# A hybrid SSM and attention layer on one core: input projections in another order, with gate tiles in the scan and in the attention

## The chip, the core and the metric

One NeuronCore of a Trainium2 chip runs the whole program. The metric is device time in microseconds (us) of one execution, the median of three. The engines are TensorE (PE; its weight loads are PEld), VectorE (DVE), ScalarE (ACT), GpSimd (POOL) and SyncE (SP). They run their own instruction streams and meet at semaphores. ACT and SP also issue the DMAs.

## What is computed

A prompt of 512 tokens and 8 sample sequences of 8 tokens pass through one layer with the same weights: 576 tokens of width 1024.

```
h = rms_norm(x, w)
z, xBC, dt, q, k, v, gate_ssm, gate_attn = split(h @ w_in)     # 2048|4096|32|1024|256|256|1024|1024
u = silu(causal_conv4(xBC)); xs, B, C = split(u)
y = ssd_scan(xs, softplus(dt), A, B, C)          # chunks of 128, one more for the samples
y = (y + xs * d_skip) * silu(z)
A_out = group_rms_norm(y, 8 groups) @ w_ssm_out
B_out = window_attention_with_sinks(rope(q), rope(k), v) @ w_attn_out
x = x + (sigmoid(gate_ssm) * A_out + sigmoid(gate_attn) * B_out) @ w_out
x = x + peer_ffn(rms_norm(x))                     # 16384 experts, top 16 of 8 heads
out = rms_norm(x)
```

The conv state, the SSM state and the key and value windows are outputs too.

## The kernel before

Activations lie transposed, 128 channels in the partitions and 576 tokens in the free dimension. A *projection tile* is 128 output columns of a weight matrix: 8 pieces of 128 x 128, each multiplied as high and low halves in fp32r (high by high, high by low, low by high), in two column halves of 288, so 48 matmuls into two PSUM banks. `project(n, p, ...)` issues it; `n` counts weight tiles and `p` the PSUM pair (parity) and its uses.

Each weight tile goes through two buffers: SP loads it into `raw` (512 KB), ACT copies the high part (`high(n)`, `whi`), POOL subtracts for the low part (`low(n)`, `wlo`). `high(n)` waits until PE is done with tile `n-2`, and everything behind it in ACT's program waits with it. The order of the weight tiles in memory is the order of use, given by the constants `N_DT`, `N_XBC`, `N_QKV`, `N_ATT`, `N_Z`, `N_SSM`, `N_OUT`.

No scheduler is at work: each engine's order is the order in which its function is written. The stages ahead of the expert network are:

1. norm, the dt tile, then 32 conv tiles (`N_XBC`). ACT copies a tile out of PSUM (`fill`), DVE does the four taps (`conv`, L1499 to L1515), ACT the silu.
2. the scan `ssd(c)` over four prompt chunks and one sample chunk. In a chunk DVE stages the chunk's operands, PE forms the cumulated decays (L570, L571), turns six blocks (L586), and then goes through 8 groups: `front(g)` spreads the decays (L611) and multiplies C by B (L614); `back(g)` makes the chunk state (L626) and the outputs (L637, L640). Between them are ACT's exponentials (`exps`) and DVE's masks and products. In the sample chunk `new_states` (L598) and 8-column outputs (L647) take the place of the state products, and ACT moves 16 states of 512 KB in and out.
3. 12 tiles of q, k and v, with the rotation on ACT and DVE (`swap`, `rope`).
4. the attention of the prompt, 16 units (`scores` L702, softmax on DVE and ACT, `turn` L713, `take` on ACT, `values` L725), then four pairs of samples (`attend_pair`).
5. 16 tiles: for each of 8 blocks the attention gate and the attention's output projection.
6. 16 z tiles, each with a silu on ACT and a product with y on DVE (L1801), the group sums (L794), the reciprocals (L1806) and the normalized outputs in halves (`yn`, L1809 to L1815).
7. 24 tiles: for each of 8 blocks the ssm gate and two tiles of `w_ssm_out`, merged on DVE; then 8 tiles of `w_out`.

The expert network behind it takes over half of the time and has the same instructions in both kernels.

## Time and profile before

| | us |
|---|---|
| median of 3 runs (2968.07 to 2972.53) | 2969.11 |
| the profiled execution's own time | 2970.44 |
| its span, first to last instruction | 2968.6 |
| conv tiles, 45.0 to 262.7 | 217.7 |
| four prompt chunks, 281.2 to 446.0 | 164.8 |
| sample chunk, 446.0 to 609.7 | 163.7 |
| q, k, v and the values' turn, 609.7 to 694.9 | 85.2 |
| prompt attention, 694.9 to 822.4 | 127.5 |
| sample attention, 822.4 to 870.6 | 48.2 |
| gates, outputs of both branches, 870.6 to 1254.4 | 383.8 |
| the rest (w_out and the expert network) | 1714.2 |

TensorE is busy for 2768.2 us of the span (93%), DVE for 1888.6, ACT for 915.0 and POOL for 683.4. A busy TensorE is not one at its peak: small matmuls count as busy for their latency, and it runs at one of two clocks, 2.4 GHz (shown as 1.00) or 1.2 GHz (0.50). The seven stages above were cut at the first or last instruction that belongs to them.

### The profile page before, as it was taken

How to read it: one execution, taken by the hardware profiler on the slowest of the kernel's cores; microseconds unless marked ns; L12 is line 12 of the kernel's file. 1: busy time of each engine (PE TensorE's matmuls, PEld its weight loads, DVE VectorE, ACT ScalarE, POOL GpSimd, SP SyncE). 2: the span in 40 equal slices, each digit the busy share in tenths (PEclk: the TensorE clock that was granted, in tenths of full speed). 3: DMA queues.
4: the chain of work that ended last, by engine and by line, in shares of the span. 5: the costliest groups of instructions: out<-in, count | busy, mean ns of one | idle time of the engine just before them, and what ended most of it. 6: DMA issues, size and time to landing. Idle time of an engine off the chain costs nothing.

```text
span 2968.6 us, 46810 instructions
## 1 busy us (share of the span) xinstructions
PE 2768.2 (93%) x15762; PEld 2406.5 (81%) x15762; DVE 1888.6 (64%) x3749; ACT 915.0 (31%) x1527; POOL 683.4 (23%) x345
## 2 busy tenths in 40 slices
PE   6997789997779999989999999999998999999997
PEld 5996668995369999988888888887887888888886
DVE  5998874325620582227799998884667777755554
ACT  2333440044412441123333345553221211211211
POOL 1332000021003324323345423333441111100000
PEclk9998885588869999999999999999999999999999
DMA  3221002321002212312334335457999888866662
GB/s 120 78 78 62 1 0 101 117 96 50 1 27 85 78 64 78 108 66 93 113 132 146 141 149 197 179 191 278 335 342 292 290 289 289 274 196 193 190 196 83
DMA packets 253899, 430.31 MB, mean 145 GB/s; under 512 B 146912, under 2 KB 149600, under 8 KB 252384
## 3 DMA queue, kind: packets, MB, share of 16 engines
q1 hardware_dynamic: 53712, 195.58, 18.7%
q10 hardware_dynamic: 181680, 166.60, 17.0%
q0 software_dynamic: 18432, 67.12, 6.7%
q8 instruction: 48, 0.79, 0.1%
q14 instruction: 27, 0.22, 0.0%
HBM read 349.46 MB, written 81.71 MB: 145 GB/s over the span
## 4 chain that ended last, share of the span: by engine, by line
PE 47%; issue 45%; POOL 6%; DVE 1%; DMA 1%; ACTq 0%; POOLq 0%; ACT 0%; DVEq 0%; SPq 0%
PE ps L955 24%; PE ps L854 19%; POOL wlo L488 6%; PE ps L925 4%; DMA raw<-wt 1%; ACTq L1402 0%; PE ps L534 0%; POOLq L490 0%; DVE y_out L2107 0%; DVE rinv L2105 0%; ACTq L1399 0%; PE ps L905 0%; ACT whi L1021 0%; DVE onehot_i L2004 0%; DVE wlo L2025 0%
## 5 line engine op out<-in xcount | busy, mean ns | idle before, releaser
L488 POOL TENSOR_TENSOR wlo<-raw,whi 128x1024 fp32r<-128x1024 f32 x213 | 539.4, 2533 | 1502.9 <-ACT whi L1021 1502.9
L1021 ACT ACTIVATE whi<-raw 128x1024 fp32r<-128x1024 f32 x373 | 394.9, 1059 | 1478.3 <-PE ps L955 544.7
L854 PE MATMUL ps<-h_hi,whi 128*128 128x512 f32 x1024 | 403.3, 394 | 6.7 <-DVE wlo L2025 4.8
L955 PE MATMUL ps<-act_hi,whi 128*128 128x512 f32 x1024 | 399.4, 390 | 9.1 <-DVE act_lo L1450 9.1
L854 PE MATMUL ps<-h_lo,whi 128*128 128x512 f32 x1024 | 399.8, 390 | 0.0
L854 PE MATMUL ps<-h_hi,wlo 128*128 128x512 f32 x1024 | 399.5, 390 | 0.0
L955 PE MATMUL ps<-act_lo,whi 128*128 128x512 f32 x1024 | 399.2, 390 | 0.0
L955 PE MATMUL ps<-act_hi,wlo 128*128 128x512 f32 x1024 | 399.1, 390 | 0.0
L2025 DVE TENSOR_TENSOR wlo<-raw,whi 128x1024 fp32r<-128x1024 f32 x160 | 196.1, 1225 | 306.3 <-ACT whi L1021 306.3
L525 PE MATMUL ps<-h_hi,whi 128*128 128x288 f32 x1360 | 303.0, 305 | 25.5 <-DVE h_lo L1450 18.9
L525 PE MATMUL ps<-h_hi,wlo 128*128 128x288 f32 x1360 | 296.2, 300 | 0.0
L525 PE MATMUL ps<-h_lo,whi 128*128 128x288 f32 x1360 | 296.1, 300 | 0.0
L525 PEld LDWEIGHTS ps<-h_hi,whi 128*128 128x128 f32 x1360 | 223.2, 193 | 36.3 <-issue 21.2
L955 PEld LDWEIGHTS ps<-act_hi,whi 128*128 128x128 f32 x1024 | 192.7, 188 | 49.5 <-issue 9.5
L854 PEld LDWEIGHTS ps<-h_hi,whi 128*128 128x128 f32 x1024 | 193.0, 189 | 46.8 <-ACT tmp L1317 5.2
L854 PEld LDWEIGHTS ps<-h_hi,wlo 128*128 128x128 f32 x1024 | 192.9, 188 | 40.5
L955 PEld LDWEIGHTS ps<-act_hi,wlo 128*128 128x128 f32 x1024 | 192.8, 188 | 40.2
L955 PEld LDWEIGHTS ps<-act_lo,whi 128*128 128x128 f32 x1024 | 192.8, 188 | 40.1
L854 PEld LDWEIGHTS ps<-h_lo,whi 128*128 128x128 f32 x1024 | 193.1, 189 | 38.6
L525 PEld LDWEIGHTS ps<-h_hi,wlo 128*128 128x128 f32 x1360 | 224.0, 193 | 0.0
L525 PEld LDWEIGHTS ps<-h_lo,whi 128*128 128x128 f32 x1360 | 223.9, 193 | 0.0
L2004 DVE TENSOR_SCALAR onehot_i<-consts_sb,expert_turned 128x128 f32<-128x128 f32 x512 | 205.8, 461 | 0.0
(282 smaller groups left out, 4068.2 us busy)
## 6 DMA issues: line engine op xcount, KB each, us to landing
raw<-wt SPq DMA_DIRECT2D x245, 512.0 KB, 3.2
raw<-pv SPq DMA_DIRECT2D x128, 512.0 KB, 4.5
activations<-tmp ACTq DMA_DIRECT2D x128, 256.0 KB, 2.0
gates_dense<-g_block ACTq DMA_DIRECT2D x8, 4096.0 KB, 13.1
g_tile<-gates_dense ACTq DMA_DIRECT2D x128, 256.0 KB, 3.6
gelu<-activations ACTq DMA_DIRECT2D x128, 256.0 KB, 4.1
state_s<-s_in ACTq DMA_DIRECT2D x16, 512.0 KB, 4.2
ssm_s<-state_s ACTq DMA_DIRECT2D x16, 512.0 KB, 2.9
```

What stands on the lines that cost most here:

```text
L488: pool.tensor_tensor(lo, raw[n.par][:, :], hi.bitcast(F32), ALU.subtract).then_inc(split_ready, 1)
L525: mm = pe.matmul(PS[2 * p.par + h][:, 0:HT], w[slot][:, k, :], x[:, k0 + k, h * HT:(h + 1) * HT], start=first and k == 0 and w is whi and ...
L854: mm = pe.matmul(PS[2 * p.par][:, :], w[slot][:, k, :], x[:, k, 0:SEQ], start=k == 0 and w is whi and x is HH, stop=k == KD - 1 and w is wlo)
L925: mm = pe.matmul(PS[4 + k][:, q * P:(q + 1) * P], OJ[buf][:, q, :], AI[buf][:, q, :], start=True, stop=True)
L955: mm = pe.matmul(PS[d][:, :], w[s][:, d, :], x[b][:, :], start=first and w is whi and x is ACH, stop=last and w is wlo)
L1021: act.activation(whi[slot][:, :, :].rearrange("p k c -> p (k c)"), raw[slot][:, :], ACT.Copy)\
L2004: ins = dve.tensor_scalar(AI[buf][:, q, :], iota, EJT[:, 0, tok], EJT[:, 2, tok], ALU.is_equal, ALU.mult)
L2025: dve.tensor_tensor(lo, raw[slot][:, :], hi.bitcast(F32), ALU.subtract).then_inc(split_ready, 1)
```

## The change

The 100 projection tiles between the dt tile and `w_out` are the same, in another order:

- The 12 tiles of q, k and v stand among the conv tiles: two conv tiles, one of these, twelve times, then 8 conv tiles. Rotated q and k, and v, are stored in a DRAM tensor `qkv_turned`, and loaded back by four DMAs ahead of the attention.
- The 32 gate inputs (16 z, 8 attention gates, 8 ssm gates) become *side tiles*. They use PSUM banks 0 and 1 only, and are issued in two halves of 24 matmuls (`side(n, j, part)`). ACT copies each to SBUF and stores it in a DRAM tensor `gate_inputs`.
- 20 side tiles stand in the scan, four in each chunk: a half behind the second and the fourth of the turned blocks, and a half behind the outputs of each of the groups 1 to 6. Two stand behind the scan, four in the prompt attention (a half behind every second `turn`), two in the sample attention (a half behind each pair), four behind the attention's output projection.
- To free the banks, a prompt chunk's decays use banks 2 and 3, the C by B product bank 6 alone, and the chunk state bank 7 alone; the chunk state now follows the group's outputs. The attention's scores use banks 2 and 3 alone.
- All silu(z) and products with y are done between the scan and the attention, from tiles loaded back. The group sums and reciprocals stand beside the attention's output projection, and the normalized outputs (`yn`) behind all of them. The gates are loaded back and put through the sigmoid.

```diff
+            for k in range(6):
+                mixed(Idx(N_MIX + k))
+            with pe.Fori(1, MIXES) as r:
+                for k in range(6):
+                    mixed(Idx(N_MIX + k, r, 6))
+            for k in range(CX - 4 * MIXES):
+                mixed(Idx(N_XTAIL + k))
+            def side(n, j, part):
+                if part == 0:
+                    pe.wait_ge(split_ready, n.v + 1)
+                    if not isinstance(j, int) or 0 < j < SIDES_2:
+                        pe.wait_ge(side_used, j)
...
+                slot = slot_of(n)
+                for k in range(4 * part, 4 * part + 4):
+                    for w, x in ((whi, HH), (whi, HL), (wlo, HH)):
+                        for h in range(2):
+                            mm = pe.matmul(PS[h][:, 0:HT], w[slot][:, k, :], x[:, k, h * HT:(h + 1) * HT],
...
                     mm.then_inc(turned, 1)
+                    if q in (1, 3):
+                        fill(q // 2)
...
-                        pe.wait_ge(cb_ready, u - 1)
                         pe.wait_ge(seg_ready, u - 1)
                         pe.wait_ge(ec_ready, u - 1)
...
                     mm.then_inc(y_ready, 1)
+                    if not sample:
+                        if not start or g >= 1:
+                            pe.wait_ge(cs_used, u)
+                        pe.matmul(PS[7][:, 0:4 * HP], BTK[:, g, :], XDD[:, 4 * g * HP:4 * (g + 1) * HP],
+                                  start=True, stop=True).then_inc(cs_ready, 1)
...
                     back(g)
+                    if 1 <= g <= 6:
+                        fill(g + 1)
...
+            for j in range(SIDES_1, SIDES_1 + 2):
+                for part in range(2):
+                    side(Idx(N_SIDE + j), j, part)
+            pe.wait_ge(qkv_in, 16 * 4)
...
                 turn(u)
+                if u % 2 == 0:
+                    j = SIDES_1 + 2 + u // 4
+                    side(Idx(N_SIDE + j), j, u // 2 % 2)
                 if u < UNITS - 2:
                     scores(u + 2)
...
+            for m in range(KD):
+                project(Idx(N_AO + m), Idx(P_AO + m), OH, OL)
+                group_sums(m)
+            for j in range(SIDES_2, SIDES):
+                for part in range(2):
+                    side(Idx(N_SIDE2 + j - SIDES_2), j, part)
+            pe.wait_ge(side_used, SIDES)
+            def ssm(n, p, first=False):
+                if first:
+                    pe.wait_ge(yn_done, NG // 2)
+                project(n, p, YH, YL, last=False)
+                if first:
+                    pe.wait_ge(yn_done, NG)
+                project(plus(n, 1), p, YH, YL, k0=KD, first=False)
...
+            def side(n, j, k, half):
+                high(plus(n, 2))
...
+                for h in range(2):
+                    ins = act.activation(SIDE[k][:, h * HT:(h + 1) * HT], PS[h][:, 0:HT], ACT.Copy)
+                ins.then_inc(side_used, 1)
+                act.wait_ge(side_used, j + 1)
+                act.dma_start(dram(side_dram, j), SIDE[k][:, :]).then_inc(side_out[k], 16)
...
+            for m in range(CI):
+                if m + 3 < CI:
+                    if m:
+                        act.wait_ge(yz_ready, m)
+                    load_z(m + 3)
+                act.wait_ge(z_in[m % 4], 16 * (m // 4 + 1))
+                act.activation(ZB[m % 4][:, :], ZB[m % 4][:, :], ACT.Silu).then_inc(zs_ready, 1)
+                if m == CI // 2:
+                    side_at(Idx(N_SIDE + SIDES_1 + 1), SIDES_1 + 1)
...
+            for m in range(CI):
+                dve.wait_ge(zs_ready, m + 1)
+                x = UX[:, m, :]
+                dve.tensor_tensor(x, x, ZB[m % 4][:, :], ALU.mult).then_inc(yz_ready, 1)
+            dve.wait_ge(qkv_in, 16 * 4)
...
+            for m in range(KD):
+                att(m)
+                rinv(m)
...
+            for g in range(NG):
+                yn(g)
```

TensorE in a prompt chunk, one of the groups 1 to 6, before (`seg`, `xdt` and `state` are operands of the outputs; two rows of outputs stand for eight):

```order
L611 MATMUL ps<-consts_sb,da_chunk 128x128 x4
L614 MATMUL ps<-u_bc,st_b 128x128
L626 MATMUL ps<-xdt_decayed,b_tok 128x256
L637 MATMUL ps<-seg_107,xdt 64x128
L640 MATMUL ps<-c_decayed_109,state 64x128
```

and now:

```order
L667 MATMUL ps<-consts_sb,da_chunk 128x128 x4
L678 MATMUL ps<-u_all,st_b 128x128
L695 MATMUL ps<-seg_114,xdt 64x128
L698 MATMUL ps<-c_decayed_116,state 64x128
...
L714 MATMUL ps<-xdt_decayed,b_tok 128x256
L595 MATMUL ps<-h_hi,whi_51 128x288 x2
L595 MATMUL ps<-h_lo,whi_51 128x288 x2
L595 MATMUL ps<-h_hi,wlo_53 128x288 x2
```

The chunk state (L626, now L714) moved behind the outputs, and 24 matmuls of a half side tile (L595) follow it, ahead of the next group's decays.

ScalarE behind the scan's last state store, before (the rotation's tables and the masks, then the first tile of q):

```order
L1142 DMA cos_sin<-ropes 128x1152
L1143 DMA mask_prompt<-amask 128x512
L1144 DMA mask_sample<-smask 128x1536
L1021 ACTIVATE whi_52<-raw_50 128x1024
L1154 ACTIVATE rope_swap_138<-ps 32x288 x8
```

and now (`z_148` to `z_151` are the four buffers for the z tiles):

```order
L1275 DMA q<-qkv_turned 128x8x576
L1276 DMA mask_prompt<-amask 128x512
L1277 DMA mask_sample<-smask 128x1536
L1280 DMA z_148<-gate_inputs 128x576
...
L1085 ACTIVATE whi_52<-raw_50 128x1024
L1178 ACTIVATE side_64<-ps 128x288 x2
L1181 DMA gate_inputs<-side_64 128x576
L1280 DMA z_151<-gate_inputs 128x576
L1293 ACT_TABLE_LOAD
L1293 ACTIVATE z_148<-z_148 128x576
L1280 DMA z_148<-gate_inputs 128x576
L1293 ACTIVATE z_149<-z_149 128x576
```

The loads of q and the masks stand ahead of the first z tile, and from then on a load and a silu take turns, 16 times.

TensorE in the prompt attention, before (a `turn`, the scores of the unit after next, the values):

```order
L713 MATMUL ps<-consts_sb,scores_142 128x128 x8
L702 MATMUL ps<-k_pad,q 128x256 x4
L725 MATMUL ps<-p_turned,v_tok 64x512 x2
```

In every second unit a half side tile of 24 matmuls now stands between the `turn` and the scores.

## Rows read from the trace of the kernel before

**Rows 1.** Busy time by stage: us, each engine's busy us (x instructions), clock, DMA.
```profile
45.00:262.70 217.70, 211.44 (x1548) 207.82 (x1546) 200.24 (x346) 75.20 (x160) 78.47 (x32) 0.99 0.21 75
281.20:446.00 164.80, 130.06 (x1009) 102.97 (x1009) 124.25 (x293) 69.48 (x200) 0.00 (x0) 0.82 0.01 2
446.00:609.70 163.70, 153.69 (x942) 141.64 (x942) 65.58 (x108) 12.34 (x50) 0.00 (x0) 0.50 0.30 105
609.70:694.90 85.20, 80.91 (x592) 80.43 (x591) 26.08 (x50) 46.18 (x96) 28.68 (x12) 0.97 0.28 98
694.90:822.40 127.50, 93.92 (x320) 50.05 (x321) 80.74 (x162) 50.33 (x176) 0.00 (x0) 0.83 0.04 12
822.40:870.60 48.20, 33.53 (x272) 24.99 (x272) 17.54 (x84) 8.57 (x40) 0.00 (x0) 0.54 0.08 23
870.60:1254.40 383.80, 378.56 (x2752) 374.03 (x2752) 141.62 (x125) 115.40 (x167) 134.90 (x55) 0.99 0.22 75
```
**Rows 2.** Timeline, ScalarE's high parts of two weight tiles: start, us, operation, idle before.
```profile
887.14 1.06 ACT L1021 ACTIVATE whi<-raw 128x1024 fp32r<-128x1024 f32 x1 [3.27 <-PE ps L525]
893.54 1.06 ACT L1021 ACTIVATE whi<-raw 128x1024 fp32r<-128x1024 f32 x1 [5.34 <-PE ps L525]
```
**Rows 3.** Timeline of TensorE, the second prompt chunk.
```profile
321.84 0.64 PE L570 MATMUL ps<-da_chunk,consts_sb 128*128 128x32 f32 x2 [3.43 <-DVE da_chunk L1559]
...
331.18 2.05 PE L611 MATMUL ps<-consts_sb,da_chunk 128*128 128x128 f32 x8 [0.97 <-DVE b_tok L1577]
...
337.38 0.45 PE L637 MATMUL ps<-seg,xdt 128*64 128x128 f32 x4 [1.67 <-DVE c_decayed L1605]
...
347.44 1.16 PE L611 MATMUL ps<-consts_sb,da_chunk 128*128 128x128 f32 x8
...
349.55 0.45 PE L637 MATMUL ps<-seg,xdt 128*64 128x128 f32 x4 [0.30 <-DVE c_decayed L1605]
...
350.62 1.16 PE L611 MATMUL ps<-consts_sb,da_chunk 128*128 128x128 f32 x8
```
**Rows 4.** Busy time in two single microseconds: the seventh number is the clock.
```profile
320.00:321.00 1.00, 0.00 (x0) 0.00 (x0) 1.00 (x2) 0.00 (x0) 0.00 (x0) 0.96 0.00 0
614.00:615.00 1.00, 1.00 (x8) 1.00 (x8) 0.00 (x0) 0.00 (x0) 0.00 (x0) 0.77 0.70 194
```
**Rows 5.** Timeline of TensorE, one group of the sample chunk.
```profile
474.46 1.97 PE L611 MATMUL ps<-consts_sb,da_chunk 64*128 64x64 f32 x8
...
476.95 7.19 PE L598 MATMUL ps<-xdt_decayed,b_by_seq 64*128 64x128 f32 x32
...
492.90 1.97 PE L611 MATMUL ps<-consts_sb,da_chunk 64*128 64x64 f32 x8
```
**Rows 6.** Timeline, one product of y and silu(z) without POOL, one with it.
```profile
1090.07 0.75 DVE L1801 TENSOR_TENSOR u_x<-u_x,tmp 128x576 f32 x1
...
1091.89 2.34 POOL L488 TENSOR_TENSOR wlo<-raw,whi 128x1024 fp32r<-128x1024 f32 x1 [4.01 <-ACT whi L1021]
1092.57 2.28 DVE L1801 TENSOR_TENSOR u_x<-u_x,tmp 128x576 f32 x1 [1.75 <-ACT tmp L985]
```
**Rows 7.** Timeline of ScalarE: a DMA issue among eight, and the silu of a z tile.
```profile
695.22 0.47 ACTq L1170 DMA_DIRECT2D v_cache<-vc  x1
...
1003.30 0.69 ACT L985 ACTIVATE tmp<-ps 128x288 f32<-128x288 f32 x2
```
**Rows 8.** The page's DMA list: tensor, queue, count, KB each, us from issue to landing.
```profile
gates_dense<-g_block ACTq DMA_DIRECT2D x8, 4096.0 KB, 13.1
```
**Rows 9.** TensorE's waits in the two attentions: total, times, longest.
```profile
PE ps L753 <- DVE q_sample L1748: 5.0, 4, 1.9
```
**Rows 10.** Timeline of DVE: the last but one reciprocal, and the normalization of a group.
```profile
1094.77 3.74 DVE L1806 RECIPROCAL rinv<-rinv 128x576 f32<-128x576 f32 x1
...
1098.70 1.55 DVE L1809 SCALAR_TENSOR_TENSOR yn<-u_x,params_sb,rinv 128x576 f32<-128x576 f32 x2 [0.19 <-DVE rinv L1806]
...
1102.02 0.76 DVE L1815 TENSOR_TENSOR y_lo<-yn,y_hi 128x576 f32 x1
```

**Rows 11.** Timeline of TensorE, the sums of one group in the z stage.
```profile
1002.14 2.10 PE L794 MATMUL ps<-sqz,ones 128*128 128x288 f32 x8
```

More of the change, by code:

```diff
@@ L330, in build @@
         ML = put(m_r, "m_lo", [P, KD, T], F32R)
+        RG = put(over(r2, 18432), "group_rinv", [P, NG, T])
         z_r = over(x_r)
@@ new lines, in value @@
+            def value(n, j, k):
+                high(plus(n, 2))
+                act.wait_ge(rope_done, 9 + k)
+                if k == 0:
+                    store_turned(9, 1)
+                halves(RS[k], n, ACT.Copy).then_inc(slot_used[n.par], 1)
+                act.wait_ge(slot_used[n.par], n.half + 1)
+                act.dma_start(dram(qkv_dram, j), RS[k][:, :]).then_inc(q_out[k], 16)
+            for k in range(2):
+                conv_pair(Idx(N_MIX + 3 * k), 2 * k, first=k == 0)
+                swap(Idx(N_MIX + 3 * k + 2), k, k, first=True)
@@ L1158, in _, with load_z @@
-            for k in range(2):
-                swap(Idx(N_QKV + k), k, k, first=True)
-            with act.Fori(1, 5) as i:
-                for k in range(2):
-                    swap(Idx(N_QKV + k, i, 2), i * 2 + k, k)
-            for k in range(2):
-                n = Idx(N_QKV + 10 + k)
-                high(plus(n, 2))
-                halves(VT[k], n, ACT.Copy).then_inc(slot_used[n.par], 1)
+            def load_z(m):
+                act.dma_start(ZB[m % 4][:, :], side_dram[m]).then_inc(z_in[m % 4], 16)
@@ new lines, in _, with load_gate, ssm_gate @@
+            for m in range(KD):
+                high(Idx(N_AO + m + 2))
+                z_std(m)
+                if m < KD - 1:
+                    z_squares(m + 1)
+            for j in range(SIDES_2, SIDES):
+                side_at(Idx(N_SIDE2 + j - SIDES_2), j)
+            def load_gate(m, k):
+                act.dma_start(TMP[k][:, :], dram(side_dram, m + (CI + KD))).then_inc(gate_in[k], 16)
+            def ssm_gate(n, m, k, half, first=False, last=False):
+                act.wait_ge(gate_in[k], half * 16 + 16)
+                act.activation(TMP[k][:, :], TMP[k][:, :], ACT.Sigmoid).then_inc(sgate_ready, 1)
+                for j in range(2):
+                    high(plus(n, 2 + j))
+                if not first:
+                    act.wait_ge(merged, m)
+                if not last:
+                    load_gate(m + 1, 1 - k)
```

462 lines of the change are left out of this document (242 added, 220 removed).

## Prediction, made before the kernel was run

> **What bounds the kernel now.** I read the table by stage first [rows 1]. In every stage with projection tiles TensorE is busy nearly throughout, at the full clock. Two neighbouring tiles start 893.54 - 887.14 = 6.40 us apart [rows 2], which is 48 matmuls of 0.133; a half side tile is 3.2 us. The conv stage runs at 217.7 / 33 = 6.6 us a tile, because DVE is busy for 200 of its 217.7 us. TensorE loses time elsewhere: in the prompt chunks it is busy for 130 of 164.8 us, in the attentions for 94 of 127.5 and 34 of 48.2, and the sample chunk, where it is busy nearly always, ran at the lower clock, 0.50 [rows 1]. The number of matmuls doesn't change. So the change can win only what a side tile costs less in the scan and the attentions than 6.40 us, and it loses what new waits it makes. The stages are followed one by one.
>
> **Conv stage.** 12 tiles are moved in: +76.8. A rotated tile is light for DVE, whose conv work no longer sets the pace: 24 conv tiles at 6.4 instead of 6.6, so -4. **+73.**
>
> **Prompt chunks.** A group takes 350.62 - 347.44 = 3.2 us [rows 3], set by the chain through ACT and DVE. TensorE shows 0.30 us idle in it (ahead of 349.55), and 0.2 to 0.3 more lie in its latencies; its matmuls need about 2.6. So a half tile there is hardly hidden: 2.6 + 3.2 = 5.8 us a group, in six groups 34.8. ACT and DVE need under 4 us from a group's decays to its outputs, so they keep up with that. The chunk's start is better cover. From the first matmul (321.84) to the first decays (331.18) are 9.3 us at the lower clock, with TensorE waiting for DVE. With two half tiles in it I work out 17.4: at the full clock 0.6 + 6 x 0.9 + 6.4 = 12.4, 2.7 for the cold first part, and 2.3 for b_tok's copy. The clock there was seen to fall after TensorE had been idle since 318.4 (0.96 within 320 to 321 [rows 4]), and that gap stays; the dense half tile should raise it. Then 4.9 from the decays to the first output (337.38 - 331.18 = 6.2 with decays at the lower clock, 1.3 less at the full one), 1.4 and 0.9 for the outputs of groups 0 and 7, and 5.3 for DVE's staging: 3.6 as now, and 1.7 because POOL now works in the scan. A product on DVE that took 0.75 us alone took 2.28 when it began 0.7 us into a POOL subtraction of 2.34 [rows 6]: DVE stands until POOL is done. Sum 17.4 + 4.9 + 1.4 + 34.8 + 0.9 + 5.3 = 64.7 a chunk, 259 for four, against 164.8: **+94**, where 16 tiles elsewhere cost 102. Bounds: 60 a chunk (+75) if no start is cold, 68 (+107) if POOL and the cold clock meet at both ends.
>
> The Trainium skill ("SBUF — State Buffer", "Who interferes with whom") says that DVE is held up by GpSimd only where it reads two SBUF operands or runs in a two-port mode. The row agrees, since u_x and tmp both lie in SBUF. By that rule the copies of b_tok out of PSUM would go free, and the four chunks would take some 9 us less; no row here tells.
>
> **Sample chunk.** A group takes 492.90 - 474.46 = 18.4 us [rows 5] at the lower clock, all of it TensorE. At 1.2 GHz 288 columns take 0.24 us, so a half tile of 24 matmuls is 5.8 us and a group 24.2. What the clock does decides this stage. The row of the projection behind the scan says that the clock rises about 4.6 us after dense work began (begun at 609.7, 0.77 within 614 to 615 [rows 4]). So it should rise in or behind each half tile and hold through the decays and the 7.2 us of new states, both cold work of 9.5 that then takes half, and drop somewhere in the 8-column outputs, which have no such row. Bounds: no gain (24.2 a group) and full clock throughout (12.1). I take 8 us saved, 16.2 a group, nearer to what the continuous new states suggest. Sample chunk: 163.7 + 2 (two half tiles in its start, one of them behind a wait) - 4 (group 0 warm) + 4 (POOL) - 6 x 2.2 = 152.5: **-11**.
>
> **Between scan and attention.** Before: 85.2, of which 76.8 are tiles. Now two tiles are left (12.8) and two other chains are longer. The last state's store must land (3.5 us after the scan, as now). Then ACT issues 4.6 MB for q, k, v and the masks ahead of the first z tile; 4 MB took 13.1 us in this trace [rows 8], so the first z arrives about 20 us after the scan. From there silu, product, load take turns: ACT may load tile m+3 only when DVE has multiplied m-1. So each of 12 tiles costs 0.69 + 0.75 + 0.47 + 0.1 = 2.0 us [rows 6, 7], and with the last four, a side tile in the middle and two POOL subtractions the loop takes 32. Copies of k and v behind it add 3: 20 + 32 + 3 = 55, against 85.2. **-30**, so of 10 tiles' 64 us more than half is given back as an idle TensorE. Bounds 45 and 62.
>
> **Prompt attention.** The half tile falls in the time in which TensorE waits; 127.5 - 93.9 = 34 us are idle [rows 1] and 25.6 come in. The chain goes from DVE's softmax to ACT and back, and scores are asked for some 5 us after the turn, so most is hidden. Not hidden: the first, at the lower clock (+3), and four POOL subtractions that catch DVE on the chain (4 x 1.6). **+9**, bounds 0 and +26.
>
> **Sample attention.** A half tile at the lower clock (5.8, some of it raised: 5.1), of which the wait for the queries covers 5.0 / 4 [rows 9], four times with the last uncovered: 3 x 4 + 5 + 2 for POOL. **+19**, bounds +10 and +26.
>
> **Outputs.** 28 tiles leave: -179.2. New waits: 2 for the copy of the last side tile; 4.4 at the third output tile, whose `high` stands in ACT behind the loads of 2.4 MB of gates and two sigmoids; 2 for the last side tile; and `yn`. That starts when the eighth reciprocal is done, 6.6 us after the last output tile (2.9, and 3.74 [rows 10]), and takes 8 x 4.1 = 33 us (1098.70 to 1102.78 [rows 10]), plus some 5 x 2.2 for POOL: 51 (2.9 is the sum on TensorE and the root on ACT). TensorE needs the second half of it after 1.9 + 25.6 + 2 + 6.4 = 36. So it waits 15. That makes 23 us of waits. The same account of the stage before leaves 10: 383.8 less 56 tiles of 6.40 and eight group sums of 1.9 (2.10 with the last one's latency [rows 11]), which stand in both. So +13. **-166**, bounds -178 and -158.
>
> Behind that nothing changes. Sum: 73 + 94 - 11 - 30 + 9 + 19 - 166 = **-12**. The profiled execution's span is 2968.6 and its own time 2970.4, 1.3 above the median; so 2969.1 - 12 = **2957**.
>
> **Rivals.**
>
> *The clock stays low in the sample chunk* (slower than before). If the half tiles don't raise it, or it drops at once behind them, six groups cost 24.2 instead of 16.2: +48, 3005; half of that gives 2981. For it: 164 us in which TensorE was busy 94% of the time at 0.50 [rows 1], new states of 7.2 us without a rise among them. Against it: rows 4, where a projection raised the clock in less time than the half tile has. It decides against the change from a group of 18.2 us on (-12 + 6 x 2 = 0).
>
> *The clock stays high through the sample chunk.* Groups near 13 us: -25, **2932**. The Trainium skill ("TensorE: Matmul & The Clock Gate", "What's actually happening") says that activity releases the throttle and a sustained busy engine gets the full clock. By that this would hold. The sample chunk of this trace disagrees, since it is busy and at 0.50; the rule needs a narrower sense of busy than the profile's.
>
> *DVE and ACT are less late than worked out.* If the z loop overlaps (1.3 us a tile) and `yn` isn't held by POOL, -8 and -11: **2938**. For it: my loop adds up latencies that the trace shows only in other places.
>
> *The change does nothing where it says most*: in the prompt chunks the half tiles find no room (0.5 us a group). That is in the sum; were the starts as bad as the groups, +8, 2965.
>
> **Chances.** Forecast 0.50 (its own range 2940 to 2972), clock low 0.22 (2972 to 3010), clock high 0.13, less late 0.15. The likeliest gives 2957. The range reaches from 2920, for two of the better cases together, to 2995, short of the full price of the low clock. A measurement here tells about 0.2% (6 us) from no change. Faster by more than that (below 2963): 0.28 of the forecast's 0.50, and nearly all of the two better cases: 0.60. Within 0.2%: 0.16. Slower: 0.24.
>
> **What would show it.** Right: a prompt chunk of 62 to 67 us; the granted clock of the sample chunk between 0.6 and 0.9 and its length near 152; the first scores some 55 us behind the scan with TensorE idle for about 40; a single wait of TensorE of about 15 us for y_lo. Wrong: a clock of 0.50 in the sample chunk, groups above 6.5 us in the prompt chunks (then a chain through ACT, which now waits for tiles among its exponentials, is the bound), or a prompt attention over 150 us.

## The result, and the profile after

The changed kernel takes **2984.5 us** (median of 6 runs, 2977.2 to 2993.7) against 2969.3 of the kernel before; the ratio is 1.0051, 95% interval 1.0036 to 1.0065. So it is slower by half a per cent, where 2957 was forecast. The profiled execution has a span of 2984.0, 15.4 more than that of before. One execution in the slow state (4805.5 us, in experiment 1) is left out of all that follows.

The stages of the new kernel, as [rows 1] shows those of the old one (busy us and number of instructions of TensorE, its weight loads, VectorE, ScalarE, GpSimd; granted clock; DMA share; GB/s):

```profile
45.00:338.10 293.10, 285.59 (x2119) 285.19 (x2118) 206.58 (x396) 123.07 (x257) 105.83 (x44) 0.98 0.28 91
338.10:351.10 13.00, 1.09 (x15) 0.81 (x13) 11.24 (x26) 4.25 (x7) 2.34 (x1) 0.70 0.27 93
351.10:606.20 255.10, 221.93 (x1776) 207.14 (x1776) 133.23 (x293) 96.16 (x248) 37.74 (x16) 0.93 0.15 50
606.20:797.90 191.70, 168.14 (x1134) 156.92 (x1134) 67.04 (x108) 18.95 (x62) 9.40 (x4) 0.64 0.32 110
797.90:849.00 51.10, 18.74 (x111) 18.27 (x110) 15.49 (x26) 15.18 (x23) 4.71 (x2) 0.67 0.66 225
849.00:984.40 135.40, 113.00 (x514) 75.48 (x516) 81.19 (x162) 57.82 (x189) 9.44 (x4) 0.90 0.11 35
984.40:1052.30 67.90, 51.09 (x369) 43.17 (x369) 19.85 (x86) 11.89 (x46) 2.96 (x2) 0.67 0.10 29
1052.30:1269.00 216.70, 201.63 (x1408) 196.85 (x1408) 111.88 (x107) 60.69 (x80) 70.55 (x28) 0.96 0.30 96
```

Set against [rows 1], stage by stage:

| stage | before | after | change | forecast |
|---|---|---|---|---|
| conv tiles | 217.7 | 293.1 | +75.4 | +73 |
| wait ahead of the scan | 18.5 | 13.0 | -5.5 | 0 |
| four prompt chunks | 164.8 | 255.1 | +90.3 | +94 |
| sample chunk | 163.7 | 191.7 | **+28.0** | **-11** |
| between scan and attention | 85.2 | 51.1 | -34.1 | -30 |
| prompt attention | 127.5 | 135.4 | +7.9 | +9 |
| sample attention | 48.2 | 67.9 | +19.7 | +19 |
| outputs | 383.8 | 216.7 | -167.1 | -166 |
| the rest | 1714.2 | 1715.0 | +0.8 | 0 |

(The wait ahead of the scan lies between 262.7 and 281.2 in the kernel before, between two rows of [rows 1].) One stage missed its forecast by 39 us. All others together came out 12 us below theirs. The question for the runs is what happened in the sample chunk.

One group of the sample chunk, in TensorE's timeline of the changed kernel (start, us, operation; in brackets the idle time before it and what ended it), to be read beside [rows 5]:

```profile
676.71 0.85 PE L595 MATMUL ps<-h_hi,whi 128*128 128x288 f32 x2
...
682.16 1.10 PE L667 MATMUL ps<-consts_sb,da_chunk 64*128 64x64 f32 x8
...
683.45 4.12 PE L655 MATMUL ps<-xdt_decayed,b_by_seq 64*128 64x128 f32 x32
687.50 0.33 PE L695 MATMUL ps<-seg,xdt 64*64 64x64 f32 x2
692.06 1.88 PE L705 MATMUL ps<-c_decayed,state_s 128*64 128x8 f32 x16 [4.24 <-DMA state_s<-s_in]
...
698.68 1.87 PE L705 MATMUL ps<-c_decayed,state_s 128*64 128x8 f32 x16
705.98 1.10 PE L667 MATMUL ps<-consts_sb,da_chunk 64*128 64x64 f32 x8
```

The half tile (676.71 to 682.16) starts a pair of matmuls every 0.48 us up to 681.20, and only its last three pairs are closer (0.26 to 0.36 us). The decays then take 1.10 instead of 1.97 and the new states 4.12 instead of 7.19. But the first 8-column outputs wait 4.24 us for a load of states, an idle time that the kernel before doesn't have, and run at 1.88 as ever. The clock over the same stretch, in three pieces (columns as above):

```profile
676.40:680.80 4.40, 4.40 (x21) 4.38 (x21) 3.94 (x6) 0.00 (x0) 0.00 (x0) 0.50 0.00 0
680.80:687.80 7.00, 6.95 (x53) 6.25 (x52) 2.93 (x6) 3.14 (x9) 2.35 (x1) 0.96 0.34 119
687.80:704.80 17.00, 12.76 (x89) 12.30 (x89) 4.57 (x8) 0.00 (x0) 0.00 (x0) 0.51 0.36 123
```

So of a group of 23.8 us (682.16 to 705.98) some 7 are at 2.4 GHz. The waits of TensorE in the chunk (total, times, longest), and the page's DMA list (count, KB each, us to landing), which has 4.2 us for these loads in the kernel before:

```profile
PE ps L705 <- DMA state_s<-s_in: 19.3, 5, 5.1
```

```profile
state_s<-s_in ACTq DMA_DIRECT2D x16, 512.0 KB, 5.9
```

### The profile page after: what moved, and what is told of

Same layout as the page of the kernel before. It is cut to its first block, busy times and chain, and to the rows that moved or that the text cites. A ratio compares the mean times of both kernels' runs of the same rounds, so it can differ in the third digit from the quotient of the medians.

```text
span 2984.0 us, 46325 instructions
## 1 busy us (share of the span) xinstructions
PE 2744.6 (92%) x15762; PEld 2406.5 (81%) x15762; DVE 1862.8 (62%) x3749; ACT 920.8 (31%) x1542; POOL 684.2 (23%) x345
## 3 DMA queue, kind: packets, MB, share of 16 engines
q10 hardware_dynamic: 194128, 192.56, 19.3%
## 4 chain that ended last, share of the span: by engine, by line
PE 46%; issue 45%; POOL 6%; DVE 1%; DMA 1%; ACTq 0%; POOLq 0%; ACT 0%; DVEq 0%; SPq 0%
PE ps L1018 23%; PE ps L917 19%; POOL wlo L508 6%; PE ps L988 4%; DMA raw<-wt 1%; ACTq L1530 0%; PE ps L554 0%; POOLq L510 0%; DVE y_out L2234 0%; DVE rinv L2232 0%; PE ps L968 0%; ACT whi L1085 0%; DVE onehot_i L2131 0%; ACTq L1527 0%; DVE wlo L2152 0%
## 5 line engine op out<-in xcount | busy, mean ns | idle before, releaser
L917 PEld LDWEIGHTS ps<-h_hi,whi 128*128 128x128 f32 x1024 | 193.0, 189 | 47.5 <-ACT tmp L1445 5.4
L917 PEld LDWEIGHTS ps<-h_hi,wlo 128*128 128x128 f32 x1024 | 192.9, 188 | 40.5
L917 PEld LDWEIGHTS ps<-h_lo,whi 128*128 128x128 f32 x1024 | 193.1, 189 | 38.4
L545 PE MATMUL ps<-h_hi,whi 128*128 128x288 f32 x848 | 187.5, 303 | 28.4 <-DVE h_lo L1578 21.6
L545 PE MATMUL ps<-h_lo,whi 128*128 128x288 f32 x848 | 184.7, 300 | 0.0
L545 PE MATMUL ps<-h_hi,wlo 128*128 128x288 f32 x848 | 184.4, 300 | 0.0
L545 PEld LDWEIGHTS ps<-h_hi,whi 128*128 128x128 f32 x848 | 138.7, 192 | 34.4 <-issue 22.8
L545 PEld LDWEIGHTS ps<-h_lo,whi 128*128 128x128 f32 x848 | 139.8, 193 | 0.0
L595 PE MATMUL ps<-h_hi,whi 128*128 128x288 f32 x512 | 132.2, 344 | 8.3 <-issue 6.2
## 6 DMA issues: line engine op xcount, KB each, us to landing
activations<-tmp ACTq DMA_DIRECT2D x128, 256.0 KB
g_tile<-gates_dense ACTq DMA_DIRECT2D x128, 256.0 KB, 3.7
gelu<-activations ACTq DMA_DIRECT2D x128, 256.0 KB, 3.6
```

The lines of the kernel that those rows point to most:

```text
L545: mm = pe.matmul(PS[2 * p.par + h][:, 0:HT], w[slot][:, k, :], x[:, k0 + k, h * HT:(h + 1) * HT], start=first and k == 0 and w is whi and ...
L595: mm = pe.matmul(PS[h][:, 0:HT], w[slot][:, k, :], x[:, k, h * HT:(h + 1) * HT], start=k == 0 and w is whi and x is HH, stop=k == KD - 1 a ...
L917: mm = pe.matmul(PS[2 * p.par][:, :], w[slot][:, k, :], x[:, k, 0:SEQ], start=k == 0 and w is whi and x is HH, stop=k == KD - 1 and w is wlo)
```

## The experiments

Below, TensorE's work is called *cold* where it runs at 1.2 GHz and *warm* where it runs at 2.4. The theory after this reading: the sample chunk costs 39 us more than forecast since (a) the raised clock gives some 4 us a group and not 8, and (b) TensorE waits 19.3 us for states, because the half tile stands where it delays the new states, whose results must be stored before the buffer is loaded again, with three buffers in turn. The rival: the clock alone, or the half tiles as such, wherever they stand. (The reason given in (b) proved too narrow; what delays the loads is read from ScalarE's timeline in the part on the sample chunk below.)

### 1. The half tile ahead of the outputs

```
             new_states(g, 0)
+            if 1 <= g <= 6:
+                fill(g + 1)
             pe.wait_ge(mt_ready, u + 1)
...
                 back(g)
-                if 1 <= g <= 6:
-                    fill(g + 1)
```

> The changed kernel, but in groups 1 to 6 of the sample chunk the half side tile stands between the new states and the outputs instead of behind the outputs. Theory (place): the half tile then covers the loads of the states (waits of 4.24 + 1.77 + 5.09 + 3.62 + 4.60 = 19.3 us in the changed kernel), and it still raises the clock, now for the outputs in place of the decays and new states (about 4 us less a group either way). Groups of about 20 us instead of 22.7, sample chunk about 175 instead of 191.7, no wait for a state load; total about 2968. Rival (the clock alone): the 8-column outputs don't gain from the clock and the decays and new states are cold again: groups 18.4 + 5.8 = 24.2, total about 2993.

Measured: 2972.3 us (median of 9), 12 less than the changed kernel, ratio to the kernel before 1.0008 (0.9998 to 1.0018). The sample chunk takes 179.8 us, 12 less as well, with groups of 20.5 on average (637.72 to 740.47, five groups), and no wait for a load is left. Its TensorE timeline:

```profile
681.81 7.19 PE L655 MATMUL ps<-xdt_decayed,b_by_seq 64*128 64x128 f32 x32 [0.18 <-DVE state_s L1789]
...
694.41 1.10 PE L707 MATMUL ps<-c_decayed,state_s 128*64 128x8 f32 x16
...
697.27 1.87 PE L707 MATMUL ps<-c_decayed,state_s 128*64 128x8 f32 x16
```

New states are cold again (7.19), and the first two of the four pieces of outputs are warm or nearly so (1.10 and 1.25 instead of 1.87; in another group all four are): this is the duration at the full clock that no row of before had. The clock gives no more here (24.2 - 20.5 = 3.7 us a group) than where the half tile stood before (groups of 22.9 with 2.2 of wait in each on average, so 24.2 - 20.7 = 3.5), and the kernel is still 12 us faster. So the place of the half tile matters, through the loads, and the "clock alone" rival (2993) falls.

### 2. A fourth buffer for the states

```
+        S0.append(nc.alloc_sbuf_tensor_at("state_s3", [P, SB, P], F32, offset=tmp_at - 4096))
...
-                    if 1 <= v < 2 * NG - 2:
-                        act.wait_ge(s0_out[(v - 1) % 3], 16 * ((v - 1) // 3 + 1))
-                        load_states(v + 2)
+                    if 1 <= v < 2 * NG - 3:
+                        act.wait_ge(s0_out[(v - 1) % 4], 16 * ((v - 1) // 4 + 1))
+                        load_states(v + 3)
```

> The changed kernel with a fourth buffer for the sample states, each load issued one state earlier; nothing else moved. Theory: the waits of TensorE for state loads (19.3 us in five groups) go and nothing takes their place: all groups at about 21 us, sample chunk about 173, total about 2966. Rival: the loads are only slower because the weight tiles are loaded beside them, and one buffer more moves the wait to the stores or to DVE's updates: half or less of it goes, 2975 or more.

Measured: 2965.5 (median of 10), 19 less than the changed kernel, ratio to before 0.9986 (0.9973 to 0.9999). The chunk takes 169.8, the waits for loads fall from 19.3 to 5.4. TensorE in one group, and the clock of its two parts:

```profile
680.32 1.10 PE L668 MATMUL ps<-consts_sb,da_chunk 64*128 64x64 f32 x8
...
681.61 4.12 PE L656 MATMUL ps<-xdt_decayed,b_by_seq 64*128 64x128 f32 x32
...
685.91 1.10 PE L706 MATMUL ps<-c_decayed,state_s 128*64 128x8 f32 x16
...
690.18 1.88 PE L706 MATMUL ps<-c_decayed,state_s 128*64 128x8 f32 x16 [1.63 <-DMA state_s<-s_in]
```

```profile
680.32:688.80 8.48, 8.18 (x81) 7.45 (x80) 3.39 (x6) 3.13 (x9) 2.35 (x1) 1.00 0.62 181
688.80:699.00 10.20, 8.82 (x54) 8.65 (x55) 4.03 (x6) 0.00 (x0) 0.00 (x0) 0.51 0.35 137
```

The wait did two things. It stood between the new states and the outputs, and in some groups it kept the outputs out of the time at the full clock: in the changed kernel the clock stood at 1.00 for the first 3.0 and 2.9 us of the waits that end at 737.69 and 760.34, though only for some 0.2 us of the one shown above. With most of the wait gone, the first half of the outputs shown runs warm. The groups from 662.11 on take 18.2, 19.5, 18.2 and 19.6 us. That is a group of before with a half tile in it at nearly no cost. The chunk's remaining 6 us against 163.7 are mostly the first filled group, 24.2 (24.5 in the changed kernel). So the late loads do cost these 19 us, and (a) and (b) are not independent. But the edit adds a buffer and also issues each load one state earlier in ScalarE's program, and it doesn't tell which of the two was needed. The loads still take 5.9 us to land, against 4.2 in the kernel before: that they are slower is so, but it doesn't keep the gain away.

### 3. The sample chunk's tiles behind the scan

```
-                    if q in (1, 3):
+                    if q in (1, 3) and not sample:
                         fill(q // 2)
...
                         back(g)
-                        if 1 <= g <= 6:
-                            fill(g + 1)
...
-            for j in range(SIDES_1, SIDES_1 + 2):
+            for j in range(CI, SIDES_1 + 2):
                 for part in range(2):
                     side(Idx(N_SIDE + j), j, part)
```

(The half tiles of groups 1 to 6 are taken out of the sample chunk alone; ScalarE's part of the tiles moves too, three ahead of the z loop and three at its steps 2, 5 and 8.)

> The changed kernel with the four side tiles of the sample chunk moved behind the scan, where TensorE idles for 29.5 us waiting for the z loop and the copies of k and v: six tiles there instead of two. Theory: the sample chunk goes back to the 163.7 us of the kernel before (-28), and the stage behind it grows by less than 5 us since four tiles (25.6) fit into the idle time: about 2960. Rival: ScalarE, which takes the tiles' copies and high parts between the z tiles, stretches the z loop, and the stage grows by 15 or more: 2972 or more.

Measured: 2979.2 (median of 10), ratio to before 1.0030 (1.0018 to 1.0043). The sample chunk is nearly back, at 165.8, 26 less. The stage behind takes 74.3 instead of 51.1. The rival holds in its size, not in its reason. TensorE there:

```profile
803.15 0.50 PE L595 MATMUL ps<-h_hi,whi 128*128 128x288 f32 x2 [1.84 <-ACT side L1176]
813.12 0.51 PE L595 MATMUL ps<-h_hi,whi 128*128 128x288 f32 x2 [1.84 <-ACT side L1176]
```

A side tile costs 10.0 us here, not 6.4: all side tiles use the same pair of PSUM banks, so each waits for ScalarE to copy the one before, and after the idle time of 1.8 to 2.1 us the clock falls, just behind the start of the tile: for the tile begun at 783.20 it reads 0.50 in the microseconds from 784 to 786, and 1.00 from 787 on.

### 4. The same with two pairs of banks

```
+                    bank = (j + 1) % 2
+                    pe.wait_ge(side_used, j - 1)
...
-        mm = pe.matmul(PS[h][:, 0:HT], w[slot][:, k, :], x[:, k, h * HT:(h + 1) * HT],
+        mm = pe.matmul(PS[2 * bank + h][:, 0:HT], w[slot][:, k, :], x[:, k, h * HT:(h + 1) * HT],
```

> The kernel with the sample chunk's four side tiles moved behind the scan, and there the six tiles take turns between two pairs of PSUM banks. With one pair they started 10.0 us apart, since each waited 1.84 us for ScalarE's copy of the one before and then ran its first 3 us at the lower clock. Theory: back to back they take 6.4 each (some 40 us), the z loop and the copies of k and v end the stage again at about 52 us instead of 75.8: total about 2958. Rival: ScalarE's part of the tiles (a copy, a high part and a store, 2.1 us each, and its waits for them) stretches the z loop: still 65 us or more, 2970.

Measured: 2966.5 (median of 10), ratio 0.9985 (0.9976 to 0.9995), between the two forecasts. The six tiles now start at 774.21 and are done by 816, with one hole of 2.08 us (a low part that came late, as ScalarE made its high part late), but TensorE then waits longer:

```profile
774.21 0.82 PE L604 MATMUL ps<-h_hi,whi 128*128 128x288 f32 x2 [0.83 <-issue]
...
809.70 0.53 PE L604 MATMUL ps<-h_hi,whi 128*128 128x288 f32 x2 [2.08 <-POOL wlo L510]
...
835.28 3.78 PE L770 MATMUL ps<-k_pad,q 64*128 64x256 f32 x8 [17.40 <-DVE k_tok L1832]
```

The stage takes 61.9 (12 less than with one pair of banks, and 11 more than in the changed kernel), and what ends it is the z loop (by way of the copies of k and v), which runs on ScalarE in turns with the tiles' own work. Theory and rival are both right in part: TensorE had room for the tiles; ScalarE, whose timeline stops for each of them, did not.

### 5. No side tiles in the sample attention

```
-SIDES_1, SIDES_2 = 20, 28
+SIDES_1, SIDES_2 = 20, 26
...
                     attend_pair(i, h)
-                    j = SIDES_2 - 2 + i
-                    side(Idx(N_SIDE + j), j, h)
```

> The changed kernel with the two side tiles of the sample attention moved to the outputs stage. Theory: they cost 67.8 - 48.2 = 19.6 us where they are and 2 x 6.4 = 12.8 there: total about 7 less, 2978. Rival: the outputs stage hides part of them under the wait for y_lo (about 12 us less altogether, 2972), or the wait for the states' last stores was what they covered (no gain, 2984).

Measured: 2976.5 (median of 10), 8 less. By stage, in its profiled execution: the sample attention is back at 48.6, the outputs stage has 225.8 instead of 216.7, so 9 for two tiles; the rest lay in the wait of 6.3 for `y_lo`, which the changed kernel has there and this one has not.

```profile
974.80:1023.40 48.60, 33.40 (x272) 24.92 (x272) 18.04 (x87) 8.57 (x40) 0.00 (x0) 0.51 0.08 24
1023.40:1249.20 225.80, 215.04 (x1504) 210.25 (x1504) 109.63 (x107) 64.10 (x86) 73.95 (x29) 0.97 0.31 96
```

### 6. The pieces together

Four state buffers, no side tile in the sample attention, four tiles behind the scan in two pairs of banks:

```
-                    j = SIDES_1 + 2 + u // 4
+                    j = SIDES_1 + 4 + u // 4
                     side(Idx(N_SIDE + j), j, u // 2 % 2)
```

> The changed kernel with four state buffers, no side tile in the sample attention, and four side tiles behind the scan that take turns between two pairs of banks. Theory: the costs add up: -19 for the states, -19.6 for the sample attention, and the two more tiles behind the scan are hidden by the z loop: about 2946. Rival: the tiles behind the scan show (+8 or more), or the sample chunk's gain depends on where the clock stands: 2955 or more.

Measured: **2948.1** (median of 4, 2943.8 to 2953.9), ratio 0.9931 (0.9914 to 0.9949). The sample chunk takes 168.4, the stage behind it 57.0 (5.9 more than in the changed kernel, so the two further tiles do show there), the sample attention 48.6. In the sum the costs add up to what was forecast (2946), since the sample chunk's profile shows 23 less and not 19.

### 7. The normalization started earlier

```
                 rinv(m)
+                own.wait()
+                for k in range(2):
+                    x = UX[:, m * 2 + k, :]
+                    own.mark(dve.scalar_tensor_tensor(x, x, Q[:, Q_SNW + m * 2 + k:Q_SNW + m * 2 + k + 1],
+                                                      RG[:, m, :], ALU.mult, ALU.mult))
```

(And the last four side tiles in two pairs of banks, as in experiment 4.)

> As the kernel with four state buffers and no side tile in the sample attention, and besides the multiplication of yn by the reciprocal is done in place during the output tiles, where VectorE idles 3.7 us of every 8.3, and the last four side tiles take turns between two pairs of banks. Theory: yn is ready some 12 us earlier, the side tiles take 6.4 instead of 8.3 to 9.9 each, and TensorE reaches the wait for y_lo earlier: about 10 us less than without, 2936. Rival: VectorE is late for the output tiles now (a POOL subtraction makes a 1.55 us pair longer), and the tiles give the time back: 2946.

Measured: **2934.8** (median of 4, 2929.5 to 2941.1), ratio 0.9885 (0.9865 to 0.9906), 13 less than experiment 6. From the first output tile to the last matmul on y it takes 198.9 instead of 211.4. VectorE's pair does meet GpSimd, and 3.69 stands where 1.55 would, but the time for it is there (below). How much of the 13 is the norm's and how much the banks', no run separates.

```profile
1044.25 3.69 DVE L1948 SCALAR_TENSOR_TENSOR u_all<-u_all,params_sb,group_rinv 128x576 f32<-128x576 f32 x2
...
1083.20 1.55 DVE L1948 SCALAR_TENSOR_TENSOR u_all<-u_all,params_sb,group_rinv 128x576 f32<-128x576 f32 x2
```

### 8. Two half tiles a group

Experiment 7 with a half tile behind the new states and another behind the outputs:

```
             new_states(g, 0)
+            if 1 <= g <= 6:
+                fill(2 * g)
...
-                            fill(g + 1)
+                            fill(2 * g + 1)
```

> As the kernel with the early norm, with two half tiles a group in the sample chunk (one behind the new states, one behind the outputs: seven tiles there instead of four), three behind the scan and two in the outputs stage. Theory: the clock falls some 5 to 8 us after a half tile and rises 3 to 4 us into the next, so with half tiles this close it hardly falls: decays and new states 5.5, outputs 5.9, two half tiles 3.2 to 4 each, about 19 us a group, as long as now with one half tile; two tiles fewer later, -8 of 12.8 (the rest is wait for yn): about 2928. Rival: the clock falls in each piece all the same, or the state transfers (2 MB a group beside 0.5 MB of weights) set the pace: 22 us or more a group, 2945 or more.

Measured: 2938.8 (median of 4), ratio 0.9883 (0.9865 to 0.9902), no different from experiment 7. One group, and the clock of its two parts:

```profile
701.72 1.10 PE L677 MATMUL ps<-consts_sb,da_chunk 64*128 64x64 f32 x8
...
707.05 0.54 PE L605 MATMUL ps<-h_hi,whi 128*128 128x288 f32 x2
...
710.70 1.10 PE L717 MATMUL ps<-c_decayed,state_s 128*64 128x8 f32 x16
...
716.20 0.85 PE L605 MATMUL ps<-h_hi,whi 128*128 128x288 f32 x2
```

```profile
701.72:714.80 13.08, 13.03 (x127) 12.12 (x127) 3.39 (x6) 3.14 (x9) 2.35 (x1) 1.00 0.66 224
714.80:721.98 7.18, 7.18 (x39) 7.00 (x38) 4.03 (x6) 0.00 (x0) 0.00 (x0) 0.53 0.00 0
```

A group is 20.3 us with twice the projection work in it: all of decays, new states and the first half tile (3.4 us, not 5.8) run at the full clock, and the clock falls at the end of the outputs; the second half tile is cold (716.20 to 721.98) but for its last matmuls. So the forecast of the group (19) was nearly met, and no transfer sets the pace (TensorE has no wait for states in this run). What was wrong is what it would bring. The chunk is 9.8 longer than in experiment 7, and the two tiles fewer in the outputs stage give back only 3.8 of 12.8 (195.1 against 198.9), as `yn` ends at its own time. The stage behind the scan, with one tile less, took 59.7, not less: it is the z loop's.

### 9. The half tile ahead of the outputs in the prompt chunks

> The changed kernel with the half tile of groups 1 to 6 of the four prompt chunks ahead of the group's outputs instead of behind them. Theory: place matters only where TensorE waits; in the prompt chunks a group of 6.0 us is filled by its own work (2.8) and the half tile (3.2) without an idle moment, so nothing changes: within 3 us of the changed kernel. Rival: the place decides here as in the sample chunk, since the chain over ScalarE and VectorE (3.2 us a group before) gets the half tile as cover for the outputs rather than for the next decays: 0.3 to 0.5 us a group, 7 to 12 us less.

The edit is that of experiment 1, for the prompt chunks instead. Measured: 2979.5 (median of 7), ratio 1.0032 (1.0021 to 1.0044); the changed kernel, run again beside it, 2983.4. The four chunks take 256.0 us, against 255.1 in the changed kernel. The 4 us between the medians lie within the spread of either, and not in these chunks. The order is of no matter there.

### 10. z first

```
+            for m in range(3):
+                load_z(m)
             act.dma_start(KP[:, :, WIN:WIN + T], qkv_dram[8:10].rearrange("k p t -> p k t")).then_inc(qkv_in, 16)
...
+                if m < KD:
+                    act.dma_start(QT[:, m, :], qkv_dram[m]).then_inc(q_in, 16)
```

> As the kernel with the early norm, with the first z tiles loaded ahead of k, v, q and the masks, q loaded tile by tile between the steps of the z loop, and the side tiles' copies spread over the loop. Theory: the stage behind the scan is a chain that starts with 12 to 13 us of loads (4.6 MB ahead of the first z tile) and goes on with 16 steps of 2 us: with z first the loads lie beside the steps, and the first scores come about 45 us behind the scan instead of 57.8: total about 2923. Rival: the stage is bound by its bytes (some 11 MB): then the order doesn't matter, 2932 or more.

Measured: 2931.7 (median of 4, 2923.8 to 2938.6), ratio 0.9872 (0.9848 to 0.9896), 3 less than experiment 7, which four runs each don't separate. The stage takes 52.6 instead of 57.8, so 5 of the 13 us hoped for, and the sample chunk, which was not edited, 170.1 instead of 167.0. The first product comes 14 us behind the scan, but then a step takes 2.4 and not 1.9, since one more issue stands in it, and steps with a side tile 3.6; the DMA share rises from 0.66 to 0.75, which leaves the question of how near its bytes are to a bound open.

### 11. The changed kernel again

> The changed kernel once more, unedited, to stand beside the two others on the same chip: 2977 to 2994, median about 2984, as in its first six runs.

Measured: 2983.4 (median of 4, 2977.0 to 2983.8), as before. Its profiled execution has a span of 2975.2, and the 9 us less have a place: ScalarE's high parts in the conv stage come 6.24 us apart,

```profile
301.28 1.06 ACT L1085 ACTIVATE whi<-raw 128x1024 fp32r<-128x1024 f32 x1 [3.95 <-PE ps L545]
307.52 1.06 ACT L1085 ACTIVATE whi<-raw 128x1024 fp32r<-128x1024 f32 x1 [3.95 <-PE ps L545]
```

not 6.40, so the stage is 6 us shorter, and the sample chunk takes 186.2 instead of 191.7. In the executions of experiments 5 and 9, which leave this chunk as it is, it takes 185.5 and 188.7. So one profile tells its length to some 6 us only, and the 191.7 used above is the longest of the four; the gains of experiments 1 and 2 rest on the medians, 12 and 19 us. Experiments 4, 6, 7 and 8 ran on another chip than these; the kernel before took 2970.2 there, and 2970.4 and 2969.2 here.

## Why the prediction was wrong, step by step

**Conv stage: right.** +75.4 against +73. The steady tile was 6.40 with VectorE no longer behind. The wait ahead of the scan, which the prediction left as it was, fell from 18.5 to 13.0: VectorE is busy for 11.2 us of it, where it was for 16.6. That term was missing. (In the forecast, 24 tiles at 6.4 instead of 6.6 make -4.8, not -4.)

**Prompt chunks: right.** The chunks take 63.9, 63.3, 64.2 and 63.7 (64.7 forecast), a group 6.0 (5.8). TensorE has no idle row in a group:

```profile
588.22 1.05 PE L667 MATMUL ps<-consts_sb,da_chunk 128*128 128x128 f32 x8
...
589.43 0.45 PE L695 MATMUL ps<-seg,xdt 128*64 128x128 f32 x4
...
590.85 0.61 PE L595 MATMUL ps<-h_hi,whi 128*128 128x288 f32 x2
...
594.22 1.05 PE L667 MATMUL ps<-consts_sb,da_chunk 128*128 128x128 f32 x8
```

Experiment 9 shows that the place in the group is free there. The 16 tiles cost 90.3 for 102.4 saved, as the forecast's "hardly hidden" had it.

**Sample chunk: wrong, and the whole miss.** The step was "I take 8 us saved, 16.2 a group". The five groups from 636.36 to 751.06 took 22.9 on average. Two things make the 6.7 us: 4.5 are a saving that was mis-sized, and 2.2 are waits.
- The saving was mis-sized. The decays and new states are warm, as the prediction said, and down from 9.6 us to 5.3 in the group shown; on average the clock gave 3.5 (24.2 - 20.7). The other half of the 8 was to come from the half tile itself and the outputs. But the half tile is cold for 4.5 of its 5.5 us, so that the clock serves what follows it, and the outputs stay cold. The bound "no gain" (24.2) and the bound "full throughout" (12.1) held the value; I took it nearer to the wrong one. The rival "clock stays low" was the right sign for the wrong reason: the clock is at 0.64 over the stage, inside the range that the prediction called right (0.6 to 0.9), and the time is that of "half of that gives 2981".
- The wait for states was missing altogether. The prediction counted what TensorE does in a group, and each DMA and queue in the other stages, but not here that a group moves 2 MB in and out, and that ScalarE issues these transfers in its own order, among its other work. It cost 19.3 us of idle (11.1 in the five groups, 8.2 in the last two), and experiment 2 got 19 back.

Where the load was late can be read from ScalarE's timeline, here ahead of the wait that ends at 692.06:

```profile
682.27 1.06 ACT L1085 ACTIVATE whi<-raw 128x1024 fp32r<-128x1024 f32 x1 [18.53 <-PE ps L595]
...
684.40 0.91 ACT L1215 ACTIVATE seg<-ps,a_cum 64x64 f32<-64x64 f32 x4 [0.47 <-ACT side L1178]
...
685.72 0.45 ACTq L1253 DMA_DIRECT2D state_s<-s_in  x1
```

and in the kernel before, where the outputs that need the load begin at 502.91:

```profile
496.34 0.45 ACTq L1125 DMA_DIRECT2D state_s<-s_in  x1
```

The load that TensorE waits for is issued at 685.72, 2.1 us ahead of the moment at which the outputs could start (687.82), and takes 6.3 us. It does not wait for its buffer: the state that lay in it was sent to be stored at 664.95, and such a store lands in 3.1 us. Nor does it wait for VectorE, which had updated the state ahead of it in the order by 679.75. It stands in ScalarE's program behind that state's store, and the store behind the high part of a weight tile, which waits for the end of the half tile, behind the copy of the side tile, and behind the exponentials of the group after next, which wait for the decays behind the half tile. In the kernel before, the stores and loads of a group stand ahead of these exponentials: the load is issued at 496.34, 0.4 us behind the update and 6.6 us ahead of its use. In experiment 1, where the half tile no longer lies ahead of the decays, it is issued at 683.00, 11 us ahead of the outputs at 694.16. This exchange in ScalarE's order belongs to the change (`exps(g + 2)` ahead of `move_states`), though the list of the change above doesn't name it and the prediction gave it no term. The new states, 4.12 us instead of 7.19, then shorten the time from the decays to the outputs. Every second wait is longer (4.24, 5.09 and 4.60 against 1.77 and 3.62), and these are the groups in which ScalarE has a side tile's work. Not shown is whether three buffers would do with the store and the load ahead of the exponentials, as before: no run puts them back there.

With the mis-sized saving alone the forecast would have been 2957 + 6 x 4.5 = 2984; with the waits it is 3003, less the 12 by which the other stages came out lower 2991. The start and the last group of the chunk, without their wait, took some 7 us less than forecast, which leads to the 2984 measured.

The Trainium skill ("TensorE: Matmul & The Clock Gate", "What's actually happening") has activity release the throttle. Here the rows say: in the chunk of before, with TensorE busy for 94% of the time, the clock stood at 0.50; it rose 4.5 us into a half tile; and with half tiles before and behind the outputs (experiment 8) it stayed at 1.00 for 13 us through 8-column and 128-column work. So the skill's direction is right, and its plain sense of a busy engine is not enough to tell which work counts; these runs don't tell it either.

**Between scan and attention: right in the sum.** 51.1 against 55. The z loop's step is 1.89, forecast as 2.0, and z arrives 20.5 us behind the scan, as forecast. In the timeline of ScalarE a load and a silu take turns:

```profile
818.43 0.68 ACT L1293 ACTIVATE z<-z 128x576 f32<-128x576 f32 x1 [6.46 <-DMA z<-gate_inputs]
819.93 0.34 ACTq L1280 DMA_DIRECT2D z<-gate_inputs  x1
820.32 0.68 ACT L1293 ACTIVATE z<-z 128x576 f32<-128x576 f32 x1 [1.21 <-DVE u_all L1812]
```

TensorE's idle time was 32 us, not 40: the two tiles take 9.1 and 8.0 us, a cost hidden here and shown by experiment 3.

**The attentions: right.** +7.9 and +19.7 against +9 and +19. Experiment 5 returned the second in full.

**Outputs: right by luck.** -167.1 against -166, but with other parts. The wait for `y_lo` is 6.3, not 15; in its place the last side tiles ahead of it start 9.9, 8.4 and 8.4 us apart instead of 6.4:

```profile
1130.66 0.50 PE L595 MATMUL ps<-h_hi,whi 128*128 128x288 f32 x2 [1.79 <-issue]
...
1157.34 0.53 PE L545 MATMUL ps<-y_hi,whi 128*128 128x288 f32 x2 [1.75 <-ACT side L1178]
...
1170.18 0.85 PE L545 MATMUL ps<-y_hi,whi 128*128 128x288 f32 x2 [6.34 <-DVE y_lo L1948]
```

The prediction had 2 us for the copy of the last side tile, and missed that each of them waits for the one before (1.79 us), and that behind the first of these waits the clock falls (0.50 from 1132 to 1135). Behind the next two it stays at 1.00, which is why they are 8.4 us apart and not 9.9. As `yn` sets the end, what the tiles lose the wait gives back. The mechanism behind the sum, that `yn` ends the stage, was right: experiment 8 shows it, where two tiles fewer give back only 3.8 us, and experiment 7 fits it, though its two edits are not told apart. Of the 4.4 at the third output tile only 1.6 were found.

**Chances.** Faster was given 0.60, but its parts make at most 0.28 + 0.13 + 0.15 = 0.56; the other 0.04 have no source.

## What to carry to other kernels

When a stage is filled with foreign work, list for each buffer that rotates in it the chain from its last reader through update, store and load to its next reader, and compare it with the new spacing. Look up also where each store and load stands in the program of the engine that issues it, and what that engine waits for ahead of it: here the buffer was free and the load still came late. A transfer that nobody waits for today may be hidden by the very time that you are about to save. Work that raises the clock pays only for what stands behind it, so put the part that a wait could cut off next to it, with the wait out of the way. An accumulator used by every filling tile costs a copy's latency, and often a cold start, each time it is used twice in a row; with two in turn (experiment 4) both went. Where an engine's chain sets the end (here `yn`, and the z loop), moving tiles about on TensorE moves only idle time.

## What the runs showed of the hardware

- The 8-column outputs follow the clock: 16 of them take 1.87 us at 1.2 GHz and 1.10 at 2.4. The kernel before has only the first.
- In the sample chunk the clock rose 4.5 us after a half tile began (676.71 to 681.2). How long it then held was not the same from group to group: behind the changed kernel's first half tile it fell in the midst of the new states (about 664.3, 3.4 us behind the half tile), in the one shown at about 688, with the wait for states; in experiment 2 at about 689, in a wait again, and at about 706 among outputs; in experiments 1 and 8 among outputs without any wait. With a second half tile in between it held for 13 us.
- Behind an idle time of 1.8 us between two dense tiles the clock fell in some cases and not in others. In experiment 3 it fell each time (1.84 us idle, then 0.50 for 3 to 4 us, and tiles 10.0 us apart); in the changed kernel's outputs stage it fell behind the first of three such idle times of 1.79 us and not behind the other two (9.9, 8.4 and 8.4 us apart).
- A DMA that an engine issues waits with the engine: the load of a state above was issued at 685.72, though its buffer had been free since about 668 (a store issued at 664.95, and 3.1 us to land), since ScalarE had stood for 18.53 us until the end of TensorE's half tile.
- The same kernel's conv stage ran at 6.40 us a tile in one profiled execution and at 6.24 in another, at a granted clock near 1 in both; experiment 5's execution shows 6.24 too. No run tells why, and it accounts for 6 us of the spread between executions.
